# Hybrid decoder step on one core: first projection chunk in four pieces, a block end without a wait for its stores, and one store moved to ScalarE's queue

## What is computed

```python
# layer 0
z, xbc, dt = split(x @ w_in, [2048, 2048 + 3072])      # x: 320 x 1024, w_in: 1024 x 5152
xbc, new_conv = causal_conv(xbc, conv_state, conv_w, conv_b)
y, h = ssd_scan(...)                                    # and the states of the samples
mix = (rms(y * silu(z)) * norm_w) @ w_out
# layer 1: latent attention in place of the above
# both layers
x = layer_norm(alpha * x + mix, ...)
aff = sigmoid(x @ router)                               # top group of 4, then top 2 experts of 8 in it
out = sum over experts of gate * (silu(x @ w_gate) * (x @ w_up)) @ w_down
x = layer_norm(alpha * x + out, ...)
```

## Time and profile before

| | us |
|---|---|
| median of 3 runs | 1233.32 (1232.72 to 1233.38) |
| the profiled execution | 1232.86 |
| its span | 1231.1 |
| TensorE (PE) busy | 1095.7 (89% of the span) |
| VectorE (DVE) busy | 452.8 |
| ScalarE (ACT) busy | 228.6 |
| GpSimd (POOL) busy | 145.0 |
| mean granted clock of TensorE | 0.937 |
| moved by the core's 16 DMA engines | 311.96 MB, mean 253 GB/s |

### The profile page before, as it was taken

The page is one execution under the profiler, slowest core; times in us unless marked ns, Lnnn a source line. Parts: engine busy times, 40 slices in busy tenths (PEclk is TensorE's granted clock), DMA queues, the critical chain, the costliest instruction groups (busy, mean ns, idle before and its releaser), DMA issues. The chain is left out here.

```text
span 1231.1 us, 14040 instructions
## 1 busy us (share of the span) xinstructions
PE 1095.7 (89%) x4918; PEld 567.0 (46%) x4918; DVE 452.8 (37%) x1165; ACT 228.6 (19%) x550; POOL 145.0 (12%) x213
## 2 busy tenths in 40 slices
PE   6999996778899997999988688899999999998884
PEld 4777775556533453333333254555564433333321
DVE  0017775674655554212211352323202632121116
ACT  0101112221300221112111132312112221121112
POOL 0000000361000001111110014041000101111100
PEclk9999997876799998999999978999999999999988
DMA  5333267000236497999999676257137689999993
GB/s 224 137 136 135 86 274 284 1 1 35 108 145 247 160 395 293 410 423 423 424 424 421 238 277 219 84 163 282 35 117 293 266 350 425 424 423 422 423 385 125
DMA packets 54046, 311.96 MB, mean 253 GB/s; under 512 B 12962, under 2 KB 13858, under 8 KB 33122
## 3 DMA queue, kind: packets, MB, share of 16 engines
q1 hardware_dynamic: 42722, 298.56, 60.8%
q0 software_dynamic: 11264, 12.61, 3.1%
HBM read 300.61 MB, written 33.59 MB: 271 GB/s over the span
## 5 line engine op out<-in xcount | busy, mean ns | idle before, releaser
L1341 PE MATMUL ps<-ring,xsT 128*64 128x512 f32 x704 | 163.7, 619 | 23.4 <-DMA ring<-in_experts 19.1
L412 PE MATMUL ps<-XT,ring 128*128 128x320 f32 x640 | 174.0, 435 | 11.4 <-DMA ring<-in_w_in 11.4
L412 PEld LDWEIGHTS ps<-XT,ring 128*128 128x128 f32 x640 | 122.4, 191 | 62.5 <-issue 12.4
L1341 PEld LDWEIGHTS ps<-ring,xsT 128*64 128x64 f32 x704 | 55.3, 142 | 129.0 <-issue 119.9
L1694 DVE TENSOR_TENSOR work<-work,ps 128x256 f32<-128x256 f32 x32 | 13.5, 421 | 269.6 <-ACT work L1423 269.6
L1368 PE MATMUL ps<-ring,hT 128*64 128x512 f32 x352 | 80.4, 598 | 1.5 <-ACT hT L1427 0.9
L1341 PE MATMUL ps<-hi,xsT 128*64 128x512 f32 x320 | 74.3, 618 | 6.9 <-DMA hi<-in_experts 6.9
L1488 POOL DMA_INDIRECT y_dram<-ys,index x32 | 32.1, 1004 | 375.1 <-DVE ys L1726 339.1
L1266 PE MATMUL ps<-C 128*128 128x512 f32 x140 | 71.5, 630 | 0.6 <-PEq L2096 0.3
L1480 POOL DMA_INDIRECT XT<-x_dram,index x32 | 32.8, 1025 | 321.4 <-DMA x_dram<-X 147.8
L1423 ACT ACTIVATE work<-ps 128x256 f32<-128x256 f32 x32 | 12.3, 384 | 274.5 <-PE ps L1341 274.5
(11 more groups left out here) (343 smaller groups left out, 1421.6 us busy)
## 6 DMA issues: line engine op xcount, KB each, us to landing
ring<-in_experts SPq DMA_DIRECT2D x36, 2048.0 KB, 24.2
ring<-in_experts SPq DMA_DIRECT2D x60, 1024.0 KB, 21.5
hi<-in_experts SPq DMA_DIRECT2D x20, 2048.0 KB, 24.3
ring<-in_w_in SPq DMA_DIRECT2D x10, 2048.0 KB, 7.8
hi<-in_experts SPq DMA_DIRECT2D x20, 1024.0 KB, 27.1
ring<-in_latent SPq DMA_DIRECT2D x60, 256.0 KB, 4.2
ring<-in_w_out SPq DMA_DIRECT2D x4, 2048.0 KB, 15.1
ring<-in_state SPq DMA_DIRECT2D x4, 1024.0 KB, 8.7
```

The source lines that it names most:

```text
L412: mm = pe.matmul(ps[:, q, 0:TOK], ring[:, u, k * 512 + q * P:k * 512 + (q + 1) * P], XT[:, k, :], start=(k == 0), stop=(k == KD - 1))
L1341: mm = pe.matmul(ps[e * SLOTS:(e + 1) * SLOTS, GU[p], :].rearrange("p (g f) -> p g f", g=2), xsT[:, p, k, e * SLOTS:(e + 1) * SLOTS], w[:, ...
```

## The change

Four things. First, the loads of `XT` and of chunk 0 are cut along the contraction into four pairs of DMAs, 320 KB and 512 KB, each pair with a semaphore `first_in`; TensorE runs chunk 0 with k as the outer loop over the four banks and waits for a pair only before the first of its two k. Chunk 1 is written out behind it, and the loop covers chunks 2 to 9. Second, `cvo` becomes a part of `lnp[:, 1, :]`, and SP's two waits at the block's end go: `cvo_out` is waited for by SP before it loads `lnp` in `states_and_output`, `y_cleared` by VectorE before it writes `yS`. Third, the store of the sample rows is issued by ScalarE, between the sigmoid's table load and its four column blocks, in both layers. Fourth, since SP no longer waits for `norm_set` before that store, its load of expert 5 stands first in the block; in layer 0 it still waits for the two gathers.

```diff
                 @block.sync
                 def _(sp):
-                    sp.dma_start(XT[:, :, :], a["xT"]).then_inc(x_in, 16)
-                    for u in range(2):
-                        sp.dma_start(ring[:, u, 0:KD * 512], a["w_in"][u]).then_inc(chunk_in[u], 16)
+                    for i, landed in enumerate(first_in):
+                        k = slice(2 * i, 2 * i + 2)
+                        sp.dma_start(XT[:, k, :], a["xT"][:, k, :]).then_inc(landed, 16)
+                        w = slice(2 * i * 512, (2 * i + 2) * 512)
+                        sp.dma_start(ring[:, 0, w], a["w_in"][0][:, w]).then_inc(landed, 16)
+                    sp.dma_start(ring[:, 1, 0:KD * 512], a["w_in"][1]).then_inc(chunk_in[1], 16)
...
                     sp.dma_start(o["conv"], cvo[:, :, :]).then_inc(cvo_out, 16)
-                    sp.wait_ge(cvo_out, 16)
-                    sp.wait_ge(y_cleared, 16 * (2 * TOK // P))
...
-                    pe.wait_ge(x_in, 16)
-                    with pe.Fori(0, 5) as it:
+                    for k in range(KD):
+                        if k % 2 == 0:
+                            pe.wait_ge(first_in[k // 2], 32)
+                        for q in range(4):
+                            if k == 0:
+                                pe.wait_ge(freed[q], 1)
+                            mm = columns(0, q, k)
+                            if k == KD - 1:
+                                mm.then_inc(proj_done, 1)
...
+                    chunk(1, 0)
+                    with pe.Fori(1, 5) as it:
                         for u in range(2):
...
-                cvo = buf(st, "cvo", [P, XBCB, CONVO])
+                cvo = lnp[:, 1, 0:XBCB * CONVO].rearrange("p (b t) -> p b t", b=XBCB)
...
                             sp.wait_ge(y_turned, 1)
+                            sp.wait_ge(cvo_out, 16)
                             sp.dma_start(lnp[:, :, :], a["ln"][0]).then_inc(ln_in, 16)
...
+                    v.wait_ge(y_cleared, 16 * (2 * TOK // P))
...
-                    sp.wait_ge(norm_set, 1)
-                    sp.dma_start(x_dram[SAMPLE, :], X[0:ROWS[2], 2, :]).then_inc(x_out, 16)
...
                     act.activation(spare[:, 0:1], eps[:, 0:1], ACT.Sigmoid)
+                    act.wait_ge(norm_set, 1)
+                    act.dma_start(x_dram[SAMPLE, :], X[0:ROWS[2], 2, :]).then_inc(x_out, 16)
                     flipped_act(act, 0, 2)
```

More of the change, by code:

```diff
@@ L202, in program @@
         gate_up_in, down_in = sems("gate_up_in", RING), sems("down_in", RING)
-        x_out, y_cleared = sem("x_out"), sem("y_cleared")
+        x_out, y_cleared, cvo_out = sem("x_out"), sem("y_cleared"), sem("cvo_out")
         router = buf(ctx, "router", [P, KD, EXPERTS])
@@ L290, in add_rows @@
                 if t == 0 and self.layer == 0:
-                    v.wait_ge(x_in, 32)
+                    v.wait_ge(x_in, 16)
                 v.wait_ge(self.rows_done, t + 1)
@@ L364, in in_projection @@
                 chunk_in = [s("chunk_in0"), s("chunk_in1")]
-                proj_done, dt_done, conv_done, cvo_out = map(s, ["proj_done", "dt_done", "conv_done", "cvo_out"])
+                first_in = [s(f"first_in{i}") for i in range(KD // 2)]
+                proj_done, dt_done, conv_done = map(s, ["proj_done", "dt_done", "conv_done"])
                 kept = [s("kept0"), s("kept1")]
@@ L399, in _, with columns, chunk @@
                     sp.dma_start(o["conv"], cvo[:, :, :]).then_inc(cvo_out, 16)
-                    sp.wait_ge(cvo_out, 16)
-                    sp.wait_ge(y_cleared, 16 * (2 * TOK // P))
                 @block.tensor
                 def _(pe):
-                    pe.wait_ge(x_in, 16)
-                    with pe.Fori(0, 5) as it:
-                        for u in range(2):
[L408 to L415, removed]
+                    def columns(u, q, k):
+                        return pe.matmul(ps[:, q, 0:TOK], ring[:, u, k * 512 + q * P:k * 512 + (q + 1) * P],
+                                         XT[:, k, :], start=(k == 0), stop=(k == KD - 1))
+                    for k in range(KD):
[7 more added lines that the diff above has]
+                                mm.then_inc(proj_done, 1)
+                    def chunk(u, it):
+                        pe.wait_ge(chunk_in[u], 16 * (it + u))
+                        for q in range(4):
+                            pe.wait_ge(freed[q], 2 * it + u + 1)
+                            for k in range(KD):
+                                mm = columns(u, q, k)
+                            mm.then_inc(proj_done, 1)
+                    chunk(1, 0)
+                    with pe.Fori(1, 5) as it:
+                        for u in range(2):
+                            chunk(u, it)
                     pe.wait_ge(wdt_in, 16)
```

## The result

| | before | changed kernel |
|---|---|---|
| median, us | 1233.02 (4 runs) | 1215.59 (4 runs, 1214.1 to 1218.75) |
| the profiled execution | 1232.86 | 1215.21 |
| its span | 1231.1 | 1213.5 |
| mean granted clock | 0.937 | 0.943 |

The ratio is 0.9864, interval [0.9843, 0.9885]: 1.4% faster, 17.4 us. Forecast were 1218.4, or 14.9 us by the terms; the profiled execution is 17.65 us shorter than the one before.

The account below looks back on a forecast made before the run. Bounds: first-load bytes, a barrier behind a small store, and layer 0's late gather with idle DMA engines in a byte-bound layer. 1232.86 - 5.5 - 4.7 - 4.9 + 0.2 = 1217.96, median 1218.4; own range 1216 to 1221, wide 1214.5 to 1223.5.

Parts of the forecast that it names:

- Part one: Start of the projection: loading the first chunk in pieces lets TensorE start earlier, worth 5.5 us, bounds 4.1 to 6.1.
- The first lands at 5.6: Kernel start: the first pair of loads lands at 5.6 instead of TensorE's start at 11.39, a gain of 5.8 us.
- the bank order's stall: Before chunk 1: TensorE waits for ScalarE's table load and first SiLU, between 0 and 0.5 us, taken as 0.3.
- the first eight take the slow start of the records with them, as before: Chunk 0: the first eight matmuls contain TensorE's slow start as before; a pair's eight matmuls take 4.7 us.
- Rival D: Kernel start: a late first pair or pieces slower than TensorE eats them, 1.3 us instead of 5.5, 1222.6; chance 0.07.
- Part two: End of the projection: the barrier follows VectorE's last work instead of a store, worth 4.7 us, bounds 4.0 to 5.2.
- Part three: Layer 0's experts: sample store on ScalarE's queue lands in time, expert 5 goes out 4.9 us earlier, bounds 0 to 7.7.
- Rival A: Layer 0's sample store lands no earlier from another queue, so the gather starts where it did; 1223.3; chance 0.13.
- I count 4.9 and not TensorE's own lead: Layer 0's experts: bytes bound the rest of the layer, so only expert 5's earlier issue counts, 4.9 us.
- Rival B: Layer 0's end follows TensorE's lead, including 2.8 us from its clock: 7.7 instead of 4.9, 1215.6; chance 0.07.
- ScalarE's issue: Layer 0, before the four column blocks: issuing the store loses 0.2 us, or 0.8 at 1.2 us per issue.
- Rival C: ScalarE is held at its DMA until SP's backlog is worked off, 15.2 us slower, 1248.5; chance 0.05.

Follow-up runs that it names:

- p1_pieces: The kernel before with only the first chunk's loads cut into four pieces; 1226.89 us, ratio 0.9947 to the kernel before.
- w1_warm: The changed kernel with three matmuls of zeros on TensorE before the first pair has landed; 1213.70 us, ratio 0.9854 to the kernel before.
- p2_nohold: The kernel before with only SP's two waits for stores at the block's end removed and `cvo` put in `lnp`; 1226.87 us, ratio 0.9952.
- p3_store: The kernel before with only the sample store on ScalarE's queue and expert 5 first in SP's block; 1224.27 us, ratio 0.9940.
- x5_held: The changed kernel with expert 5 of layer 0 issued only when half of the first pair is done; 1221.08 us, ratio 0.9918 to the kernel before.
- x5_free: The changed kernel with expert 5 of layer 0 no longer waiting for the two gathers; 1222.36 us, ratio 0.9932 to the kernel before.
- act8: The changed kernel with eight more 16 KB stores issued by ScalarE behind the sample store, in both layers; 1227.96 us, ratio 0.9973 to the kernel before.

## Why the forecast was right, and where it was off

**Part one, forecast 5.5, measured 4.7** (at VectorE's last work; 4.9 there in p1_pieces, of which 4.4 reached the scan, since its store of `cvo` still held the block). "The first lands at 5.6" was close: 5.29, so the start gained 6.1 for 5.8. "It should not stop between them" held, and so did the bank order's stall, 0.39 for 0.3. The step that failed is "the first eight take the slow start of the records with them, as before": the slow start lasted 5.5 us and not 2.8, which made chunk 0 longer by 1.2. 6.1 - 1.2 - 0.4 = 4.5 at chunk 1. w1_warm took these slow records away and got 2.6 back. The size is partly chance: with slow starts of 3.4 to 6.0 us in the other traces, the lead at VectorE's last work was between 4.4 and 6.1, and the forecast's 5.5 lies within.

That a fixed cost per DMA would add up over the eight did not show. The list of the four loads of w_in says how long each took to land:

```profile
DMA to landing us min/median/max: 3.9/6.8/8.5
```

The last was issued at 4.16, so all were there by 12.7 us (those of `XT` took at most 7.7). The estimate that adds up the Trainium skill's cost per DMA (DMA: Bandwidth & Descriptors, "Two cost components", a fit for DMAs that GpSimd issues) over the eight had 23.8. Rival D, with 1.3, falls.

**Part two, forecast 4.7, measured 4.9** (5.0 in p2_nohold, at the scan). The order of events was as told; only the handoff was smaller, 0.30 for 0.53.

**Part three, forecast 4.9, measured 6.2 at the end of layer 0 and 6.8 at the end of the span in p3_store, 6.8 at both in the first trace.** In the other traces with this part, x5_held and x5_free aside, it is 6.6 to 7.5 at the end of layer 0. p1_pieces and p2_nohold, which don't have it, read 0.9 and 0.6 there, so about 1 us of it can be chance. The store landed in 8.1 us, between the bounds and inside the 15.7 that were left, `index` released the gather, and expert 5 followed after 4.6. Rival A falls. Of the two rules of the Trainium skill that stood behind it (DMA: Bandwidth & Descriptors), the one in "Queues, rings and completion order", by which the engines take turns between queues, agrees with the 8.1 against 19.8. "Issuing engines are not separate DMA queues", by which a second issuer saves only issue time, doesn't fit: the store landed 13.5 us sooner for standing in another queue, and the measurement decides. The step that failed is "I count 4.9 and not TensorE's own lead". Bytes do bound the layer, as x5_held shows, but the stream also ran denser behind an earlier TensorE, by 1.3 to 2.6 us. Rival B had the right neighbour, and the price of the clock was as it said (the next loads are called 2.7 us sooner behind the turn of the rows, for its 2.8); but the layer's end does not follow TensorE, and the measured value lies between the two.

**ScalarE's issue, forecast 0.2, measured 0.** The sum put it behind the table's small activation; it ran beside the table load. Rival C falls by act8.

**The rest, 1.1 us,** is the clock in the scans (78.79 us for 79.90 before), which none of the parts touches. It was allowed for as about 1 us of TensorE's clock; single traces differ by up to 3.0 there (77.02 to 80.00), so this term is chance.

From 14.9 forecast to 17.6: -0.8 (part one), +0.2 (part two), +2.0 (part three), +0.2 (ScalarE) and +1.1 (scans). The total came out close partly because a term too high stood against others too low. That rival B's 1215.6 is the measured median is luck of the same kind: its own term, 7.7, was 0.9 too high and part one's 0.8, and the scans and the two small terms made up for them.

## What to carry to other kernels

A barrier, or the first consumer of a round trip through memory, should not wait for a small store that stands in the queue of the large loads: give it its own buffer and a wait where that buffer is next used, or issue it from another engine's queue, for about 0.5 us of that engine's time. In a stage bounded by bytes count what starts the stream, and then look whether its next loads wait for slots that the compute engine frees; here that was worth another 1.3 to 2.6 us. When adding up gains from single traces, check stages that the edit doesn't touch, here the scans and the attention, and take their difference off first.

## What the runs showed of the hardware that was not expected

- TensorE's first records are 0.53 us apart for a while, and then about 0.27. That lasted 2.8 to 3.9 us where they began at 11.4, and 3.4 to 6.0 us where they began at 5.1 to 5.8; behind idle matmuls from 2.04 the real ones at 5.40 showed none in two traces (17.54 us for 64 in w1_warm) and 2.1 us of it in a third. The granted clock reads 1.00 in this stretch, so the spacing of the records tells it and that column doesn't (windows of the changed kernel, the slow stretch and the rest of chunk 0):

```profile
5.29:10.75 5.46, 5.46 (x11) 3.53 (x11) 0.00 (x0) 0.00 (x0) 0.00 (x0) 1.00 0.98 357
10.75:25.45 14.70, 14.70 (x55) 10.07 (x53) 0.00 (x0) 1.48 (x2) 0.00 (x0) 1.00 0.64 262
```

- Eight loads of 320 and 512 KB, issued 0.46 us apart on one queue, came without a stop that TensorE could feel, the first pair 4.4 us after its issue.
- The scan stage, the same 400 records of TensorE in all 14 profiles, took 77.02 to 80.00 us, at granted clocks of 0.89 down to 0.81, and w1_warm, a changed kernel, is as slow there as the kernel before.
- The first two gathers of layer 0 needed 3.0 us to land in the changed kernel, and 9.8 in x5_free beside 3 MB of weights.
- Eight further issues on ScalarE's queue cost 0.65 us each beside a full SP queue, one alone 0.46 to 0.52, while the landings took 8.0 to 15.7; and 5.1 us of TensorE's idle behind them cost it 2.0 us more in the sixteen matmuls that followed.
